# A fused transformer kernel on one core: the gated embeddings with a split gate product, and the projection of p placed among the down products

## The reference, cut to what matters

```python
def swiglu_2(x, w_gu, w_down):                      # w_gu 1024 x 5632, w_down 2816 x 1024
    g, u = jnp.split(x @ w_gu, 2, axis=-1)
    return (jax.nn.silu(g) * u) @ w_down

for i in range(2):
    h = h + 0.5 * swiglu_2(rmsnorm_2(h, ffn1_norm[i]), ffn1_w_gu[i], ffn1_w_down[i])
    ...                                             # the mixer
    h = h + 0.5 * swiglu_2(rmsnorm_2(h, ffn2_norm[i]), ffn2_w_gu[i], ffn2_w_down[i])
    gate = jax.nn.sigmoid(rmsnorm_2(h, ple_norm[i]) @ ple_w_gate[i])              # 1024 x 1024
    h = h + gate * rmsnorm_2(p[i] @ ple_w_proj[i], ple_post_norm[i])              # p 256 x 256
```

## Time and profile before

| | |
|---|---|
| median of 3 runs | 3116.65 us (3110.8 to 3117.39) |
| the profiled execution | span of its instructions 3110.4 us; its own time outside the span is not given, and the fastest of the three runs took 3110.8 us |
| share of the span: PE, PEld | 95%, 83% |
| share of the span: DVE, ACT, POOL | 62%, 42%, 10% |
| mean granted clock of TensorE | 0.969 of full speed |
| the two stretches of the gated embeddings | about 42 us each, from 2438.1 and from 3061.2 us |

### The profile page before, as it was taken

The page is one execution under the profiler, slowest core; times in us unless marked ns, Lnnn a source line. Parts: engine busy times, 40 slices in busy tenths (PEclk is TensorE's granted clock), DMA queues, the critical chain, the costliest instruction groups (busy, mean ns, idle before and its releaser), DMA issues.

```text
span 3110.4 us, 42332 instructions
## 1 busy us (share of the span) xinstructions
PE 2960.3 (95%) x17324; PEld 2569.5 (83%) x17325; DVE 1915.4 (62%) x2144; ACT 1311.5 (42%) x1282; POOL 301.0 (10%) x228
## 2 busy tenths in 40 slices
PE   6988998887999999999999999999999999999999
PEld 4868986356888888888877998888999899976998
DVE  4474443965888888888454553785555365463553
ACT  1223331003767677766443441344444344334442
POOL 1003932840000000000000000012000000000000
PEclk8969999898999999999999999999999999989999
DMA  7844574024999999999453564433456456451562
GB/s 244 279 146 148 178 242 136 0 94 167 354 341 328 328 359 340 324 331 341 173 199 102 175 193 135 127 118 109 136 177 198 143 163 203 136 149 54 172 199 79
DMA packets 493055, 608.20 MB, mean 196 GB/s; under 512 B 37401, under 2 KB 361084, under 8 KB 492924
## 3 DMA queue, kind: packets, MB, share of 16 engines
q1 hardware_dynamic: 491600, 605.51, 58.5%
q10 hardware_dynamic: 1324, 0.80, 0.1%
HBM read 605.22 MB, written 1.05 MB: 195 GB/s over the span
## 4 chain that ended last, share of the span: by engine, by line
PE 82%; DVE 7%; DMA 4%; issue 3%; ACT 2%; POOL 2%; SPq 0%; DVEq 0%; ACTq 0%; POOLq 0%
PE bank L1155 28%; PE bank L1017 7%; PE bank L1621 7%; PE bank L1488 4%; PE bank L1492 4%; PE bank L1495 4%; PE bank L1420 3%; PE bank L1045 3%; PE bank L1544 2%; DMA ring<-in_o_exp_down 2%; PE bank L1119 1%; PE bank L1535 1%; PE bank L1425 1%; PE bank L1127 1%; PE bank L1123 1%
## 5 line engine op out<-in xcount | busy, mean ns | idle before, releaser
L2629 DVE TENSOR_TENSOR ring_r<-ring,store_area_r 128x2048 fp32r<-128x2048 f32 (+1 forms) x336 | 783.1, 2367 | 210.0 <-ACT store_area_r L1933 209.9
L1933 ACT ACTIVATE store_area_r<-ring 128x2048 fp32r<-128x2048 f32 (+1 forms) x336 | 651.3, 1972 | 230.8 <-PE bank L1155 103.0
L1621 PE MATMUL bank<-hT,ring 128*128 128x256 f32 x1024 | 230.0, 380 | 0.0
L1155 PE MATMUL bank<-sq_r,store_area_r 128*128 128x256 f32 x1520 | 221.2, 287 | 8.4 <-ACT sq_r L1939 8.2
L3028 DVE TENSOR_TENSOR ring_r<-ring,store_area_r 128x3072 fp32r<-128x3072 f32 x64 | 195.1, 3088 | 48.0 <-ACT store_area_r L2269 48.0
L1155 PE MATMUL bank<-sq_r,ring_r 128*128 128x256 f32 x1536 | 217.2, 284 | 0.0
L1155 PE MATMUL bank<-hT_r,store_area_r 128*128 128x256 f32 x1520 | 214.2, 284 | 0.0
L1621 PEld LDWEIGHTS bank<-hT,ring 128*128 128x128 f32 x1024 | 190.8, 190 | 27.1 <-issue 3.1
L1155 PEld LDWEIGHTS bank<-sq_r,store_area_r 128*128 128x128 f32 x1520 | 198.9, 192 | 13.2 <-ACT sq_r L1939 6.5
L1155 PEld LDWEIGHTS bank<-sq_r,ring_r 128*128 128x128 f32 x1536 | 199.7, 193 | 0.0
L1155 PEld LDWEIGHTS bank<-hT_r,store_area_r 128*128 128x128 f32 x1520 | 197.1, 193 | 0.0
(11 more groups left out here) (468 smaller groups left out, 5083.3 us busy)
## 6 DMA issues: line engine op xcount, KB each, us to landing
ring<-in_o_exp_gate SPq DMA_DIRECT2D x88, 1024.0 KB, 7.1
ring<-in_o_exp_up SPq DMA_DIRECT2D x88, 1024.0 KB, 7.3
ring<-in_ffn_w_gu SPq DMA_DIRECT2D x88, 1024.0 KB, 7.5
ring<-in_o_exp_down SPq DMA_DIRECT2D x32, 1536.0 KB, 8.7
ring<-in_ffn_w_down SPq DMA_DIRECT2D x32, 1408.0 KB, 8.4
ring<-in_o_exp_down SPq DMA_DIRECT2D x32, 1280.0 KB, 11.4
ring<-in_ssd_w_in SPq DMA_DIRECT2D x32, 1024.0 KB, 7.7
ring<-in_e_mod_mix_w SPq DMA_DIRECT2D x12, 1024.0 KB, 9.2
```

What stands on the lines that cost most here:

```text
L1155: i = mm(out, w(k), x(k), start=(p == k == 0), stop=(p == 2 and k == blocks - 1))
L1621: ins = mm(dense_bank(i, s)[:, half * T:(half + 1) * T], slot(u, s, KD)[:, k, half * P:(half + 1) * P], h(k), start=(k == 0), stop=(k == K ...
L1933: activation(dst, slot(u, s, kk), ACT.Copy).then_inc(w_high, 1)
L2629: nc.vector.tensor_tensor(slot(u, s, kk, rounded=True), slot(u, s, kk), as_f(high), ALU.subtract).then_inc(w_low, 1)
```

## The change

The gate's product becomes a three-pass product like the feed-forward's, on inputs that are not yet divided by the root. The projection of p becomes one unit (4 banks' worth of output, written as two halves to one pair of banks) that stands among the down units of the feed-forward stage before: one half ahead of each half of the last down unit. So `ffn2_i` has 16 units and `ple_i` has 2. The square sums of the projection come right behind the last down unit. Three semaphores in other places are replaced by a running count, which changes no work.

```diff
-    ... ffn2_0=15, ple_0=4, ffn1_1=15, na_in=6, na_out=2, ffn2_1=15, ple_1=4)
+    ... ffn2_0=16, ple_0=2, ffn1_1=15, na_in=6, na_out=2, ffn2_1=16, ple_1=2)
...
 # SP
-                rows_halved(base[stage] + GU_UNITS, w_down, DN_UNITS)
+                for i in range(DN_UNITS):
+                    if stage[:5] == "ffn2_" and i == DN_UNITS - 1:
+                        projection_weights(int(stage[5]))
+                    rows_halved_unit(down_unit(stage, i), w_down, i)
...
 # TensorE, down(i) of ffn2
+                        if stage[:5] == "ffn2_" and i == DN_UNITS - 1:
+                            projection(int(stage[5]), t)
...
 # TensorE, ple
+                pe.wait_ge(post_sq, i + 1)
+                for k in range(KD):
+                    ins = mm(bank_x[:, 0:T], ones[:, 0:P], ffn_square(k), start=(k == 0), stop=(k == KD - 1))
+                ins.then_inc(post_sum, 1)
+                gate(0, 0)
+                raw_sums(stage)
+                gate(0, 1)
+                gate(1, 0)
+                gate(1, 1)
-                norm(stage)
-                for c in range(2):
-                    wide(Unit(base[stage] + c), 2, lambda k: pT[:, k, :])
-                wide(Unit(base[stage] + 2), KD, h, ready)
...
-                wide(Unit(base[stage] + 3), KD, h, half_done=ple_half)
...
 # ScalarE, ple
+                se.wait_ge(unit_done, projection_unit(i).at(0))
+                high(0)
+                projected(i, 1)
+                se.wait_ge(evac, projection_unit(i).at(1))
+                activation(ffn_square(0, 6), flat(y_p[:, 0:6, :]), ACT.Square)
+                activation(ffn_square(6, 2), flat(y_p[:, 6:8, :]), ACT.Square).then_inc(post_sq, 1)
+                se.wait_ge(post_sum, i + 1)
+                raw_inputs(stage)
+                activation(rs_post, bank_x[:, 0:T], ACT.Sqrt, bias=small[:, 0:1], scale=1.0 / D).then_inc(post_std, 1)
+                raw_root(stage)
+                high(1)
+                gate(0)
...
 # VectorE, the last down unit of ffn2
+                    if stage[:5] == "ffn2_" and i == DN_UNITS - 1:
+                        after = "ple_" + stage[5]
+                        ple_low(after, 0)
+                        inputs_low(after, 0, X_HEAD[after])
+                        ve.wait_ge(evac, projection_unit(int(stage[5])).at(1))
                     ve.wait_ge(unit_done, u.at(1))
                     add_to_x(u, i, gate)
...
 # VectorE, ple: scaled() multiplies a half unit by the root, gated() multiplies by the sigmoid and adds to x
+                inputs_low(stage, ffn_ahead[stage], KD)
...
+                ple_low(stage, 1)
                 tally.wait(ve)
+                for s in range(2):
+                    scaled(0, s)
+                if i == 0:
+                    first_low("ffn1_1")
+                for s in range(2):
+                    gated(0, s)
+                for s in range(2):
+                    scaled(1, s)
+                for s in range(2):
+                    gated(1, s)
```

More of the change, by code:

```diff
@@ L241, in program @@
             norm_entry(name, needs, lambda k, i=i, vec=vec: vcol(vec, 8 * i + k))
-    H_BEFORE = {name: sum(other not in ("final", "mix_1") and other[:2] not in ("ef", "ff") for other, (m, _, _) in NORMS.items() if m < n)
+    H_BEFORE = {name: sum(other not in ("final", "mix_1") and other[:2] not in ("ef", "ff", "pl") for other, (m, _, _) in NORMS.items() if m < n)
                 for name, (n, _, _) in NORMS.items()}
@@ L609, in slots_before @@
             return i * 2 + EVEN_SLOTS
-        before = sum(STAGE_UNITS[s] for s in SPLIT[:SPLIT.index(stage)])
+        before = sum(SPLIT_UNITS[s] for s in SPLIT[:SPLIT.index(stage)])
         return (i + (before + (STAGE_UNITS["moe"] if has("moe") else 0))) * 2 + EVEN_SLOTS
@@ L1817, in ple, with gate, p_turned @@
             def ple(stage):
-                i = int(stage[4])
+                i, first = int(stage[4]), base[stage]
+                def gate(c, s):
+                    u = Unit(first + c)
+                    if s == 0:
+                        banks_free(u)
+                    pe.wait_ge(w_low, slots_before(stage, c) + (s + 1))
+                    high, low = ple_high(c, s), slot(u, s, KD, rounded=True)
+                    for t in range(2):
+                        cols = slice(t * P, (t + 1) * P)
+                        w_hi, w_lo = lambda k: high[:, k, cols], lambda k: low[:, k, cols]
+                        x_hi, x_lo = lambda k: h_hi[:, k, :], lambda k: h_lo[:, k, :]
+                        ins = three_passes(banks[2 * u.r + s][:, t * T:(t + 1) * T],
+                                           ((w_hi, x_hi), (w_lo, x_hi), (w_hi, x_lo)), KD,
+                                           inputs_of(stage) if c == s == t == 0 else None)
+                    if s == 1:
+                        ins.then_inc(unit_done, 1)
+                    elif c == 1:
+                        ins.then_inc(ple_half, 1)
+                pe.wait_ge(post_sq, i + 1)
[7 more added lines that the diff above has]
+                gate(1, 1)
+            def p_turned(i):
                 pe.wait_ge(p_in, 16 * (i + 1))
```

166 lines of the change are left out of this document (99 added, 67 removed).

## The result

The changed kernel takes 3119.38 us (median of 20 runs, 3110.53 to 3140.05) against 3113.84 us before (20 runs, 3104.25 to 3119.84). The medians differ by 5.5 us (0.18%) and the means by 7.7 us. The ratio of the two kernels over all these runs is 1.0024, with a 95% interval of 1.0015 to 1.0034: the changed kernel is slower by 0.24%, about 7.5 us.

What follows compares the result with a forecast made beforehand. TensorE, busy 95% of the span, was taken as the bound; -9.1 + 2.6 + 12.0 + 1.4 + 1.2 = +8.1 us on a median of 3116.65 us gives 3124.7 us, 0.26% slower, range 3115 to 3131 us.

Steps and rivals of the forecast that it cites:

- rival 1: Gap at the gate's first pass stands, but clock holds or weights land in time: +5.1 or +2.5 us; chance 0.28.
- gate in three passes: Gate units on TensorE: 11.52 us each in three fp32r passes instead of 13.80 us; -9.1 us in both layers.
- projection and turning of p, moved: Same matmuls, now among the down products, where TensorE is the bound too: 0.
- last down unit's weights late: TensorE waits for low parts ahead of the projection, 0.6 and 2.0 us: +2.6 us, bounds nothing to 4.0 us.
- gate's inputs wait for the sums: Gate's first pass: 4.5 us of waiting plus 1.5 us of slow clock a layer, +12.0 us; bounds 4.0 to 7.0 a layer.
- hand-over to `ffn1_1`: Behind `ple_0`'s gate: rounding starts about 1.05 us later than now; +1.2 us, bounds 0.5 to 2.
- hand-over at the end: Program's end: five VectorE operations behind the last gate matmul, 3.9 us instead of 2.48; +1.4 us, bounds 0.7 to 2.
- The forecast's doubt about the clock: Clock may hold at each gate gap: +8.1 us with two falls, +6.6 us with one, +5.1 us with none.
- The transfer fit of the Trainium skill: Last down unit's weight loads: about 2.0 us plus bytes / 436 GB/s, 8.6 us from first issue; sum 2.6 us smaller.
- Rival 2: Gap of the gate's first pass hidden by roundings during the sums: -3.9 us, or -6.5 with weights in time; chance 0.07.
- Rival 3: More waits in the gate's second unit and longer at half clock: +12 us, 3129 us; chance 0.07 together with another rival.

Runs made afterwards that it cites:

- e10: e3 with the gate as one plain fp32 product again, without high and low parts; 1.0010 of before.
- e3: e1 and e2 together in the changed kernel; 0.9972 of before.
- e2: Changed kernel with the wait for the low parts of the last down unit's weights moved behind the projection's first half; 1.0030 of before.
- e1: Changed kernel with all eight gate inputs rounded ahead of the wait for the sums, only the squares of x still waiting; 1.0008 of before.
- e5: Changed kernel with unused matmuls of ones keeping TensorE busy in the gap of the gate's first pass; one profile, behind the sums 13.4 us in both layers.
- e0: The changed kernel once more, no edit; 1.0034 of before.
- e8: e4 with the high and low parts of `ffn1_1`'s first slots made ahead of the gate's sigmoids and scalings; 0.9965 of before.
- e9: e8 with unused matmuls of ones keeping TensorE busy at the start of `ffn1_1`; 0.9961 of before.
- e4: e3 with each half unit gated before the next is scaled, and `ffn1_1`'s low parts behind unit 0's gating; 0.9974 of before.
- e7: Changed kernel with only e4's order of VectorE's work behind the gate; 1.0015 of before.
- e6: Changed kernel with VectorE's addition of the last down unit ahead of the six low parts; one profile, behind the sums 14.9 and 15.9 us.

## Why the prediction was right

The forecast was 3124.7 us from a median of 3116.65 us, +8.1 us or 0.26%; measured is a ratio of 1.0024. The median came out at 3119.38 us, 5.3 us under the forecast: 2.8 us of that are the median of before, which is 3113.84 us in 20 runs. By the medians the change is +5.5 us, nearer to rival 1 (+5.1 us), and by the ratio about +7.5 us, nearer to the forecast; the times alone don't decide between the two, and the profiles do. The terms, from the profile of the changed kernel against before:

| term | predicted | measured | checked by |
|---|---|---|---|
| gate in three passes | -9.1 | -9.1 | e10: 27.6 against 23.04 us a layer |
| projection and turning moved | 0 | 0 | e3 closes without them |
| last down unit's weights late | +2.6 | +3.5 (1.6 and 1.9) | e2: gone |
| gate's inputs wait for the sums | +12.0 | +12.2 (5.7 and 6.5) | e1: gone; e5: 4.2 gap, the rest clock |
| hand-over to `ffn1_1` | +1.2 | +1.1 (2.5 in e0) | e8, e9 |
| hand-over at the end | +1.4 | +1.2 | e4, e7: half of it back |
| sum | +8.1 | +8.9 (A+B: +9.0) | |

The largest term was right in its parts too. Block 6 was forecast to be rounded 4.3 us behind the sums and was at 4.2 us (3076.61 against 3072.39). The forecast's doubt about the clock was settled: it fell at both gaps. But the sum of 6.0 us a layer hides two errors that nearly cancel: the gap itself cost 4.2 us and not 4.5 us, and the clock 1.5 and 2.3 us and not 1.5 us, by whether it was low for 3.4 us or for 6.8 us. Which of the two comes no edit sets: in layer 1 the two profiles of the changed kernel differ in it. Over the five kernels that keep this gap, *behind the sums* is 14.9 us in six of ten places (3.4 us at 0.50) and 15.6 to 15.9 us in four (6.8 us).

The term that was mis-sized most is the late weights. The forecast took the second slot's landing from rows 7 and 8, 9.9 us in layer 1 and 11.3 us in layer 0, each from its own issue, and so waits of 0.6 and 2.0 us. In the changed kernel the second high part in layer 1 starts 11.7 us behind the first issue (3040.58 against 3028.92), where the forecast had 10.3 us, and the wait is 1.9 us; in layer 0 it is 1.6 us. So both layers had the slower landing, which was the upper part of the stated bounds. It varies: *late* in layer 1 is anywhere from 0.7 to 2.0 us in the six profiles that have this wait. The transfer fit of the Trainium skill (DMA: Bandwidth & Descriptors, Anatomy of one DMA), by which there would have been no wait and which the page gives for another path, doesn't hold for these loads: 11.7 us and a wait of 1.9 us stand against the 8.6 us estimated from it.

The hand-over to `ffn1_1` was right in size by luck. The forecast had rounding start 1.05 us later than before; it starts 1.5 us later, and the first block with it. The passes behind it happened to be 0.4 us shorter than in the profile of before (8.63 against 9.03 us), which gives +1.1 us; in e0 they were 1.0 us longer, which gives +2.5 us.

Rival 1 had the gap right and the clock wrong, since it fell at both gaps: e5 shows what it would have given if the clock had held, 3.8 us less behind the sums. The forecast and rival 1 both leaned on the one profile of before, in which the clock held over 3 us of idling at the start of `ffn2_1`; in four later profiles it fell there. Rival 2 describes not this kernel but e1: with the roundings ahead of the wait the gap is 0, as its condition said. Rival 3's further waits did not come, its longer time at the low clock did in one layer; behind the sums of x the gate's units run without a wait (29.4 us from those sums to the end of the span in layer 1, of which 20.7 us are matmuls).

## What to carry to other kernels

Price a faster product together with the start that it needs. These passes save 4.6 us a layer on the bounding engine, and a single wait on ScalarE's queue, placed ahead of the roundings instead of ahead of the squares, took 6 us back; when work is moved ahead of a reduction, ask for each instruction whether it needs the reduction or only stands behind one that does. A load that is moved one unit back in a ring has lost one unit of lead, and a wait that stands ahead of independent work hides nothing. Where runs of one kernel lie 16 us apart (before, 20 runs) or 30 us (after), distances between fixed instructions in the profiles decide between theories that the times can't tell apart. Such a distance must in its turn be split until what chance sets, here the clock, stands apart from what the edit sets: the total of e8 came out as expected, though its edit did nothing there.

## What the runs showed of the hardware

TensorE's clock answered to idleness in the middle of a busy program: after 5 us in which it did eight matmuls, or within them, it stood at 0.50, half speed (1.2 GHz of 2.4), for 3.4 or for 6.8 us, and filling that gap with matmuls of no use kept it at 1.00 (e5), with a gain of 1.5 to 2.3 us for each gap. At the start of `ffn1_1` the passes behind the block-by-block start took 8.6 to 10.0 us with the clock low, and 7.7 us with fillers (e9).

The same idleness does not always lower it. The first pass of `ffn2_1` takes 3.7 us in every kernel here: four matmuls, 1.8 us of idling, and four fed one by one. The clock held at 1.00 behind it in nine of the thirteen profiles, before and after among them. In four (e0, e3, e6, e9) it fell for 3.4 us, and two of the passes took 1.5 to 1.7 us instead of 0.96 us. In e3:

```profile
2857.50:2860.70 3.20, 3.20 (x17) 3.20 (x17) 1.51 (x1) 3.20 (x2) 0.00 (x0) 0.50 1.08 343
```

Two loads of 1.4 MB that were issued together landed 7.8 and 11.7 us after the first issue in layer 1, and 6.4 and 11.4 us in layer 0 (each to the start of the work on it), though the timeline shows nothing else in the queue. Counted from its own issue, the second took 11.2 us in layer 1, and 9.9 us before the change. The rates of the changed kernel from 3028 to 3045 us, in slices of 0.425 us, show the late part of it:

```profile
GB/s 0 0 0 0 63 173 231 316 381 386 388 386 376 352 366 335 359 359 357 347 349 347 345 349 174 29 24 24 10 0 0 0 0 0 0 0 0 0 0 0
```

Nearly all bytes are there 9.7 us behind the first issue, and the last part comes at under 30 GB/s until some 11 us behind it. Why one place is slower than another stays open.
